# A quarter of the tokens of an expert layer's output taken out of the dense product: their weight rows fetched by indirect transfers and summed on VectorE

## The reference, cut to what matters

```python
def peer_ffn(h, w_query, sub_keys, expert_u, expert_v):
    ...
        sc, pos = lax.top_k(cand, PEER_TOPK)
        eidx = jnp.take_along_axis(cidx, pos, axis=-1)
        g = jax.nn.softmax(sc, axis=-1)
        u = jnp.take(expert_u, eidx, axis=0)
        a = jnp.einsum('thkd,td->thk', u, hc).astype(jnp.float32)
        act = (jax.nn.gelu(a, approximate=False) * g).astype(hc.dtype)
        vv = jnp.take(expert_v, eidx, axis=0)
        return jnp.einsum('thk,thkd->td', act, vv)
```

## Time and profile before

| | |
|---|---|
| time, median of 3 runs | 3273.46 us (3267.81, 3273.46 and 3273.85) |
| profiled execution, span from first to last instruction | 3272.9 us |
| TensorE busy | 3240.9 us, 99% of the span |
| POOL busy | 1354.7 us, 41% |
| VectorE busy | 1796.4 us, 55% |
| ScalarE busy | 1325.0 us, 40% |
| moved by transfers | 428.10 MB, mean 131 GB/s |

### The profile page before, as it was taken

How to read it: one execution, slowest core, us unless ns; L and a number is a source line. 1 busy time by engine, 2 the same in 40 slices (tenths; PEclk the granted TensorE clock), 3 DMA queues, 4 the chain that set the end, 5 groups by cost and what they waited for, 6 DMA issues and landing times.

```text
span 3272.9 us, 41516 instructions
## 1 busy us (share of the span) xinstructions
PE 3240.9 (99%) x15352; PEld 2658.7 (81%) x15352; DVE 1796.4 (55%) x3033; ACT 1325.0 (40%) x2203; POOL 1354.7 (41%) x587
## 2 busy tenths in 40 slices
PE   9999999999999999999999999999999999999998
PEld 6787778888888888888888888777888878888886
DVE  7735238998999971166666665436311145652112
ACT  5454234334777763332222223445322324543331
POOL 5520234444344344444444444354444443434442
PEclk9999999999999999999999999999999999999999
DMA  3240222344565557576666665231233331123332
GB/s 124 72 129 20 91 97 87 118 146 135 174 222 182 214 199 225 163 208 193 193 193 193 192 192 154 91 103 60 95 97 97 97 108 65 39 91 97 97 97 84
DMA packets 425115, 428.10 MB, mean 131 GB/s; under 512 B 146544, under 2 KB 344048, under 8 KB 423296
## 3 DMA queue, kind: packets, MB, share of 16 engines
q1 hardware_dynamic: 424960, 426.00, 41.7%
HBM read 354.63 MB, written 69.21 MB: 130 GB/s over the span
## 4 chain that ended last, share of the span: by engine, by line
PE 97%; DVE 1%; DMA 0%; issue 0%; ACT 0%; POOL 0%; SPq 0%; DVEq 0%; ACTq 0%
PE pb L696 29%; PE pb L697 29%; PE pb L698 29%; PE pb L1036 2%; PE pb L1268 1%; PE pb L952 1%; PE pb L930 1%; PE pb L908 1%; PE pb L795 1%; PE pb L986 0%; PE pb L918 0%; PE pb L954 0%; PE pb L1054 0%; PE pb L910 0%; PE pb L821 0%
## 5 line engine op out<-in xcount | busy, mean ns | idle before, releaser
L606 POOL TENSOR_TENSOR s_over<-s_ring,s_rhigh 128x1024 fp32r<-128x1024 f32 x517 | 1274.4, 2467 | 1840.7 <-ACT s_rhigh L1377 1840.1
L1377 ACT ACTIVATE s_rhigh<-s_ring 128x1024 fp32r<-128x1024 f32 x517 | 547.1, 1059 | 1219.3 <-DMA s_ring<-w 526.9
L696 PE MATMUL pb<-s_over,s_rhigh 128*128 128x512 f32 x2336 | 912.5, 391 | 0.1
L698 PE MATMUL pb<-s_over,s_over 128*128 128x512 f32 x2336 | 909.0, 389 | 0.0
L697 PE MATMUL pb<-s_over,s_rhigh 128*128 128x512 f32 x2336 | 908.8, 389 | 0.0
L696 PE MATMUL pb<-s_hS,s_rhigh 128*128 128x512 f32 (+1 forms) x1664 | 659.8, 397 | 4.1 <-DVE s_hS L2451 2.5
L698 PE MATMUL pb<-s_hS,s_over 128*128 128x512 f32 (+1 forms) x1672 | 646.1, 386 | 0.0
L697 PE MATMUL pb<-s_hS,s_rhigh 128*128 128x512 f32 (+1 forms) x1664 | 642.8, 386 | 0.0
L696 PEld LDWEIGHTS pb<-s_over,s_rhigh 128*128 128x128 f32 x2336 | 438.5, 188 | 92.4 <-issue 1.2
L697 PEld LDWEIGHTS pb<-s_over,s_rhigh 128*128 128x128 f32 x2336 | 438.6, 188 | 91.5 <-issue 1.2
L698 PEld LDWEIGHTS pb<-s_over,s_over 128*128 128x128 f32 x2336 | 438.5, 188 | 91.3
(11 more groups left out here) (281 smaller groups left out, 2854.0 us busy)
## 6 DMA issues: line engine op xcount, KB each, us to landing
s_ring<-w SPq DMA_DIRECT2D x272, 512.0 KB, 3.4
s_ring<-eu SPq DMA_DIRECT2D x128, 512.0 KB, 3.9
s_ring<-ev SPq DMA_DIRECT2D x128, 512.0 KB, 4.0
acts<-s_arena SPq DMA_DIRECT2D x128, 256.0 KB, 3.9
gates<-s_arena SPq DMA_DIRECT2D x8, 4096.0 KB, 13.4
s_arena<-acts SPq DMA_DIRECT2D x128, 256.0 KB, 4.2
s_arena<-gates SPq DMA_DIRECT2D x128, 256.0 KB, 4.3
s_xT<-xT SPq DMA_DIRECT2D x4, 512.0 KB, 7.4
```

The costliest lines, as they stand in the source:

```text
L606: gp.tensor_tensor(rlow[:, s, :, :], ring[:, s, :, :], rhigh[:, s, :, :].bitcast(F32), ALU.subtract).then_inc(S("w_split"), 1)
L696: mm(dst, a_high, b_high, start=start, stop=False)
L698: return mm(dst, a_low, b_high, start=False, stop=stop)
L1377: sc.activation(rhigh[:, s, :, :], ring[:, s, :, :], ACT.Copy).then_inc(S("w_high"), 1)
```

## The change

The down half is split by tokens. The first TD = 384 tokens keep the dense path, with every tile of it cut from 512 to 384 columns: the matmuls of `down`, `gated`, `act_high`, `act_low`, `add_down`, and the loads of activations and gates. The gate table is built for 384 tokens only, in 48 groups (U_GATE = TD // 8), and its DRAM layout now has one run of 384 numbers per expert.

The last 128 tokens, one per partition, are computed from the chosen rows. VectorE forms two tables of 128 x 128 integers: `s_row` has the number of each chosen expert, `s_el` the place of its activation in `acts`. For each of the 128 choices j, POOL issues two indirect transfers: `pick_act(j)` brings one activation to each partition (128 pieces of 4 bytes), and `fetch_row(j)` brings one row of `expert_v` to each partition (128 rows of 4 KB, 512 KB in all) into one of VR = 6 buffers. DVE multiplies the activations by their gates 16 at a time, and `add_row(j)` adds row j times activation j into a 128 x 1024 sum in PSUM, even j in banks 0 and 1, odd j in banks 2 and 3. The rows are spread over the down tiles r = 4 to 113. Behind them ScalarE and DVE add the two sums, TensorE turns the result by eight transposes before down tile 117, and DVE adds it to the last 128 columns of `xT`. The up half still covers all 512 tokens. Some semaphores are merged to make room.

```diff
+TD = T - P
+VR = 6
+SP0, SP1 = 4, 114
-U_GATE = 64
+U_GATE = TD // 8
+def rows_summed(r):
+    return 0 if r < SP0 else min(NK, -(-(r - SP0 + 1) * NK // (SP1 - SP0)))
+def acts_picked(r):
+    far = 16 * ((rows_summed(r - 5) + 15) // 16 + 2)
+    return min(NK, far, 16 + (3 * (r - 2)) // 2) if r >= SP0 else 0
+def rows_fetched(r):
+    return min(NK, VR + rows_summed(r - 5))
...
@@ block.gpsimd @@
-            splits(T_QUERY, T_PLE)
+            splits(T_QUERY, T_U + 120)
+            def fetch_row(j):
+                if j >= VR:
+                    gp.wait_ge(S("sp_fma"), j - VR + 1)
+                gp.indirect_dma_start(vrow[j % VR], None, rows,
+                                      bass.IndirectOffsetOnAxis(ap=s_row[:, j:j + 1], axis=0))\
+                    .then_inc(S(f"vrow{j % VR}"), 16)
+            def pick_act(j):
+                if j % 16 == 0 and j >= 32:
+                    gp.wait_ge(S("sp_mul"), j // 16 - 1)
+                gp.indirect_dma_start(s_act[:, j:j + 1], None, acts1,
+                                      bass.IndirectOffsetOnAxis(ap=s_el[:, j:j + 1], axis=0))\
+                    .then_inc(S(f"s_act{j // 16 % 2}"), 16)
+            gp.wait_ge(S("sp_idx"), 2)
+            for e in range(2):
+                gp.wait_ge(S(f"gates_out{e}"), 8 * (TD // GB))
+            for j in range(VR):
+                fetch_row(j)
+            splits(T_U + 120, T_V + RING)
+            for e in range(4):
+                gp.wait_ge(S(f"a_out{e}"), 16 * 32)
+            for j in range(16):
+                pick_act(j)
+            for r in range(RING, NK):
+                splits(T_V + r, T_V + r + 1)
+                for j in range(max(16, acts_picked(r - 1)), acts_picked(r)):
+                    pick_act(j)
+                for j in range(max(VR, rows_fetched(r - 1)), rows_fetched(r)):
+                    fetch_row(j)
@@ block.tensor @@
-            for t in range(T):
+            for t in range(TD):
...
-                    m = three(pb[:, 4 + c % 4, :], rhigh[:, n % RING, k, :], rlow[:, n % RING, k, :],
-                              actS[:, half, 0, k, :], actS[:, half, 1, k, :], k == 0, k == 7)
+                    m = three(pb[:, 4 + c % 4, 0:w], rhigh[:, n % RING, k, :], rlow[:, n % RING, k, :],
+                              av[:, half, 0, k, :], av[:, half, 1, k, :], k == 0, k == 7)
...
+                if r == 117:
+                    pe.wait_ge(S("sp_y"), 2)
+                    for c in range(DC):
+                        m = pe.transpose(pb[:, c // 4, c % 4 * P:(c % 4 + 1) * P], vrow[1][:, c * P:(c + 1) * P],
+                                         mat(M_ID))
@@ block.vector @@
+            def add_row(j):
+                if j % 16 == 0:
+                    at = slice(j, j + 16)
+                    ve.wait_ge(S(f"s_act{j // 16 % 2}"), 256 * (j // 32 + 1))
+                    ve.tensor_tensor(s_act[:, at], s_act[:, at], s_mul[:, at], ALU.mult).then_inc(S("sp_mul"), 1)
+                    ve.wait_ge(S("sp_mul"), j // 16 + 1)
+                y = pb[:, j % 2 * 2:j % 2 * 2 + 2, :].rearrange("p b n -> p (b n)")
+                ve.wait_ge(S(f"vrow{j % VR}"), 16 * (j // VR + 1))
+                if j < 2:
+                    ve.tensor_scalar(y, vrow[j % VR], s_act[:, j:j + 1], None, ALU.mult).then_inc(S("sp_fma"), 1)
+                else:
+                    ve.wait_ge(S("sp_fma"), j - 1)
+                    ve.scalar_tensor_tensor(y, vrow[j % VR], s_act[:, j:j + 1], y, ALU.mult, ALU.add)\
+                        .then_inc(S("sp_fma"), 1)
...
-                add_down(T_V + r, X_MIX + r)
+                add_down(T_V + r, X_MIX + r, w=TD)
+                for j in range(rows_summed(r - 1), rows_summed(r)):
+                    add_row(j)
```

More of the change, by code:

```diff
@@ L347, in program @@
         acts = nc.dram_tensor("acts", (NK, P, T), F32, kind="Internal").ap()
+        acts1 = acts.rearrange("n p (t one) -> (n p t) one", one=1)
+        rows = a["ev"].rearrange("n e c o -> (n e) (c o)")
+        gtab = gates.rearrange("b n p t -> (b n p t)")[0:NK * NK * TD].rearrange("(n p t) -> n p t", p=NK, t=TD)
         actS = Area().take(2, 2, 8, T, dt=F32R)
+        actE = Area().take(2, 2, 8, TD, dt=F32R)
         ga = Area(2 * 2 * 8 * T).take(2, T)
@@ L378, in program @@
         ua = C.take(4, T)
+        s_row = C.take(P, dt=U32)
+        s_el = C.take(P, dt=U32)
+        s_act = C.take(P)
+        s_tok = C.take(1)
+        s_mul = score[:, TT - 1, :, :].rearrange("p h k -> p (h k)")
         C.at = at_ch
@@ L381, in program @@
         gtile = C.take(4, T)
+        vrow = [Area(2 * 2 * 8 * TD + 1024 * i).take(1024) for i in range(4)] + [C.take(1024) for i in range(2)]
         hF = Area(ARENA - 2 * DC * T).take(2, DC, T, dt=F32R)
@@ L1000, in up, with down @@
                 m.then_inc(S("tile_done"), 1)
-            def down(n, e, x, half, g=0, step=0):
+            def down(n, e, x, half, g=0, step=0, av=actS, w=T):
                 c = (x - X_MIX) % 8
@@ L1041, in _ @@
                 up(T_U + k, k)
-            pe.wait_ge(S("gb_copied"), T // 4)
-            with pe.Fori(0, 8) as g:
+            pe.wait_ge(S("gb_copied"), TD // 4)
+            with pe.Fori(0, 7) as g:
                 for r in range(16):
-                    down(T_V + r, r // 8 * 8, X_MIX + r, r // 8, g, 16)
-            pe.wait_ge(S("p_in"), 16)
+                    down(T_V + r, r // 8 * 8, X_MIX + r, r // 8, g, 16, av=actE, w=TD)
+            for r in range(112, NK):
+                if r == 117:
[3 more added lines that the diff above has]
+                                         mat(M_ID))
+                    m.then_inc(S("sp_y"), 1)
+                down(T_V + r, r // 8 * 8, X_MIX + r, r // 8 % 2, av=actE, w=TD)
+            pe.wait_ge(S("sp_y"), 4)
+            pe.wait_ge(S("masks_in"), 48)
             for half in range(2):
@@ L1595, in _ @@
                         sc.wait_ge(S("tile_done"), g * 16 + (T_V + r))
-                    act_high(8 + r, (r // 8 + 1) % 2, r % 8, g, 16)
+                    act_high(8 + r, (r // 8 + 1) % 2, r % 8, g, 16, av=actE, w=TD)
                     m = T_V + r + 3
@@ L2197, in _ @@
                 if k >= 1:
-                    act_low(k - 1, 0, k - 1)
-            act_low(7, 0, 7)
+                    act_low(k - 1, 0, k - 1, av=actE, w=TD)
+            act_low(7, 0, 7, av=actE, w=TD)
             gated(8)
-            with ve.Fori(0, 7) as g:
-                for r in range(16):
-                    gated(9 + r, g)
-                    act_low(8 + r, (r // 8 + 1) % 2, r % 8, g, 16)
-                    add_down(T_V + r, X_MIX + r, g, 16)
-            for r in range(112, NK):
+            ve.wait_ge(S("e_read"), NK)
+            for r in range(NK):
                 if r + 9 < NK:
```

116 lines of the change are left out of this document (70 added, 46 removed).

## The result

The changed kernel takes 3318.94 us (median of 4 runs, 3314.97 to 3327.26), the one before 3272.15 (4 runs beside it): a ratio of 1.0152, with a 95% interval of 1.0136 to 1.0169. It is slower by 1.5%; I had forecast 2.5% faster, 3190 us. The profiled execution has a span of 3325.5 us against 3272.9.

What follows compares the result with a forecast made beforehand. TensorE, busy 99%, bounds the kernel before; POOL was to pace the changed down half. 3272.9 - 69.5 (down half) - 15.4 (gate table) + 0.9 (transposes) = 3188.9, stated as 3190 us, range 3115 to 3330.

Steps and rivals of the forecast that it cites:

- Gate table, 15.4 us less: Gate table stage: TensorE loses 128 matmuls of 256 columns at 0.120 us each, all 15.4 us counted as gain.
- My fourth rival: Gate table stage: DVE is the pace, so the 15.4 us gain falls away; chance 0.04, shared with cheap-form transfers.
- 384 columns every 0.173 us, tile 4.16 us: Down half, TensorE alone: 24 matmuls of 0.173 us per tile, 128 tiles in 532.5 us, 164.0 less.
- The down half, 627 us: Down half with POOL as its pace: 617 us plus 10 for waits, 69.5 less than before.
- t, 1.1 us: Down half: POOL's time to issue one indirect transfer, 250 of them, taken between 0.4 and 2.4 us.
- Rival 1: Down half: POOL's issue is cheap, under 0.8 us; DVE or TensorE sets the pace, total 3140 or 3100; chance 0.16.
- Waiting of POOL, 5.5 + 10: Down half: POOL waits 5.5 us for the last activation stores at the start, and an estimated 10 for DVE.
- Splits, 2.55 us each for 114: Down half: POOL's weight splits, between 2.40 undisturbed and 2.71 with DVE busy, 290.7 us in all.
- The end, 45.8: Down half after the last indirect transfers: TensorE does tile 117 and the last ten at 4.16 us, 45.8 us.
- 2915 + 250t: Total time in us as a function of POOL's issue time t; each tenth of a microsecond is 25 us.
- rival 2: Down half: POOL's issue is dear, kernel slower than before from t = 1.43, 3340 us at 1.7; chance 0.22.
- rival 3: Down half: transfers are the pace, 5.2 us per tile, total 3209, or dear form 7.9, total 3507; dear form 0.05.

Runs made afterwards that it cites:

- experiment 1: Changed kernel with the gate table written to and read from DRAM in the old layout: 3252.74 us, 0.9943 of the kernel before.
- experiment 2: Kernel before, with only the gate table's DRAM layout changed to the new one, write and read: 3364.65 us, 1.0276.
- experiment 8: experiment 1 without picks, rows, sums and transposes, so only the dense work remains: 3101.42 us, one run.
- Experiment 9: experiment 1 with the picks of activations given out evenly, one or two per tile, nothing left out: 3230.15 us, 0.9875.
- experiment 4: experiment 1 without the 128 transfers that pick activations, a constant in their place: 3167.57 us, one run.
- experiment 6: experiment 4 with 126 of DVE's 128 row sums only 64 of 1024 columns wide: 3138.96 us, one run.
- experiment 7: experiment 1 with DVE's sums for rows 2 to 127 only 64 of 1024 columns wide, all picks kept: 3250.58 us, one run.
- experiment 10: Changed kernel, new gate table layout written in 1 MB portions and picks given out evenly, nothing left out: 3223.83 us, 0.9856.

## Why the prediction was wrong, step by step

1. **The step that turned the sign is one that the prediction does not have.** It lists what TensorE loses in the gate table and takes the rest of the stage as it was. The diff also turns the gate table round in DRAM, and I priced neither the write nor what is queued behind it. Experiments 1 and 2 show it from both sides: 66 us in the changed kernel, 92 in the kernel before with its eight blocks. That 3319 us lie in my range of 3115 to 3330 is luck: its upper part was meant for a dear issue on POOL, and what filled it is a write that neither the sum nor a rival has.
2. **Gate table, 15.4 us less: right where the layout is taken out.** Experiment 1 has 555.3 us from the table's start to the down half against 571.5, 16.2 less. In the changed kernel it is 51.5 more. My fourth rival (DVE as the pace) had nothing in it.
3. **384 columns every 0.173 us, tile 4.16 us: right** (experiment 8). The dense stage takes 542.0, forecast 532.5; nearly 3 of the 9.5 us more are at its start, in tiles 2 and 3 with 5.6 us each.
4. **The down half, 627 us: wrong by 69.3, with POOL as the pace as forecast.** With POOL's rows of experiment 1 the sum (5.5 + 275 + 290.7 + 45.8 + 10) can be filled in term by term:
   - t, 1.1 us, was mis-sized. An instruction takes 1.01 us, but with the idle time before it 1.24 (128.6 + 124.1 busy, 57.4 idle for 250): 310.1 us instead of 275, +35.1. Rival 1's reading, that POOL's rows are two to three times longer than DVE's for the same work, is 1.9 by its own rows (1310 and 691 ns) and 2.0 for the split (2.40 and 1.21 us).
   - Waiting of POOL, 5.5 + 10, was mis-sized: 56.3 idle before splits, 54.6 of it for ScalarE, +40.8. Experiment 9 shows 24 of it to be the bursts: the prediction spread 48 picks evenly over tiles 46 to 117, and 37 of them come behind three splits. Part of the rest is the start: POOL waits 8.7 us for ScalarE's rounding there, which stands behind `act_high`, that behind `gated`, and that behind SP's load after the last store. TensorE stood 19 us before tile 4, not 9.
   - Splits, 2.55 us each for 114: 116 of 2.40 (those of tiles 2 and 3 fall into the stage too), 278.6 us, -12.1. The disturbed duration of the gate stage, half of which I had taken, does not come up here: when POOL and DVE meet in this stage, it is DVE's instruction that gets longer (`gated` 0.54 to 3.35 us in experiment 1).
   - The end, 45.8: 52.4 from the last of these splits, +6.6. TensorE itself takes 46.1 from tile 117 on, as forecast; but it starts that tile at 2001.35 us, 5 us after its split was ready, so POOL is no longer the pace there.
   The four make +70.4; the stage is 69.3 longer, the rest lies at the edges of the window.
5. **"It is 2915 + 250t", break-even at t = 1.43.** With 1.24 this gives 3225, and with all waiting in t (696 us of stage) t is 1.38. So rival 2 (dear issue, slower than before) had the right place in the down half and the right sign, but not for its reason: its price alone would not have made the kernel slower, experiment 1 is at 0.9943.
6. **The slope.** 25 us per tenth in t holds only as long as POOL is alone: experiment 4 took 160 us from POOL and gave 87.5. The second limit, which I had as rivals 1 and 3, came in as a mixture: DVE at 90%, with 30.7 us shown to be its part (experiment 6), and transfers at a share of 1.02, whose part is not shown.
7. **DVE's `add_row` 1.22 us:** 1.28 measured, from the earlier trace rows and the slope of the earlier trace rows. Costing it at nothing was right: experiment 7.
8. **Transfers, 4.2 to 5.2 us per tile:** in experiment 6 a tile takes 578.1 / 128 = 4.5 us at a share of 1.02 to 1.07. That fits; that the transfers set this pace is not shown.
9. **The issue's price and the shared port.** The Trainium skill, "DMA: Bandwidth & Descriptors", section "Latency and other measured facts", puts the first byte of a transfer from GpSimd at about 1 us. No row here shows a first byte; the instruction itself takes 1.01 us, and what the sum needs is the 1.24 us from one to the next. The Trainium skill, "SBUF — State Buffer", section "Who interferes with whom", lets a DVE instruction meet GpSimd's reads only when both its inputs are in SBUF. The trace agrees: `add_row`, with PSUM as second input, takes 1.27 to 1.29 us in all 126 cases, while `gated`, with two inputs from SBUF, has a median of 1.51 and goes from 0.54 to 3.35.

Right of the signs that I had named: idle time of TensorE before many tiles for POOL's subtraction, and tiles of unequal length, though in the changed kernel it is 5.6 us from one tile's first matmul to the next early (tiles 4 to 45) and 4.6 late (tiles 79 to 103, behind the last burst) instead of 5.2 and 4.3; with the bursts in them, tiles 46 to 117 take 5.4 in the mean. POOL waiting for ScalarE in most tiles did not come up (33 of 116 in experiment 1).

## What to carry to other kernels

When a diff changes the order of data in DRAM, price the write and the read of it as transfers of their own (length of pieces, order in DRAM, time to land), and then ask what stands behind them in the issuing queue: an urgent 512 KB tile behind 4 MB cost TensorE some 10 us of standing each time, and four portions made it nothing. Work out the table of an issue schedule by hand before predicting, because a pace that is right on average can come in bursts, and a burst longer than the ring's cover is paid twice: as a stand, and, as I read experiment 9, as an empty ring afterwards. Cost an instruction on the engine that sets the pace by the distance from start to start, not by its duration.

## What the hardware showed that I had not expected

- The issue of a weight tile by SP took 0.33 to 0.46 us around the blocks of the gate table, and 14.75 to 16.04 right behind 4 MB in 256-byte pieces; behind 1 MB of them it took 0.80 to 2.41. The 4 MB took 22.1 us to land, against 13.7 in the old layout.
- An indirect transfer of 128 pieces mostly cost POOL 0.94 to 1.1 us (means of 1003 ns for pieces of 4 bytes and 1024 for pieces of 4 KB), and there are 0.30 us of idle time before the next, about 0.15 behind a split. That is 1.24 to 1.40 us from start to start.
- TensorE's granted clock was 0.90 in stretches in which it had stood several times for 10 us (904 to 1168 us) and 1.00 in experiment 1 from 904 to 1107, without them. In the down half (1450 to 1600 and 1600 to 1800 us) it was 0.90 and 0.96 with bursts and 0.99 and 1.00 in the same windows of experiment 9, though TensorE was hardly busier (158.85 us from 1600 to 1800 against 166.15). It is not the even order alone: experiment 10, with the same order, has 0.97 to 0.98. 1.00 is the 2.4 GHz level, and a mean between 0.5 and 1.00 holds time at the 1.2 GHz level, where a matmul of 512 columns started every 0.43 us and one of 384 every 0.32. What of the gain of experiment 9 is the clock was not tried apart.
- With every third split of 128 x 1024 moved from POOL (2.40 us) to DVE (1.21), DVE's multiplications got shorter too (a mean of 1.84 to 1.19 us).
